# Expert weights in 16 KB pieces: which rows of the weights a partition holds, and the order in which turned rows take their columns

## The chip, the cores and the metric

The kernel runs on one core of a Trainium2 chip. The metric is the device time of one execution in microseconds. PE is TensorE (matmuls, with PEld for the loads of its stationary operand), DVE is VectorE, ACT ScalarE, POOL GpSimd and SP the engine that issues most DMAs. SBUF is the on-chip memory of 128 partitions; HBM is off the chip.

## What the reference computes

A decoder layer over 512 tokens of width 1024: a token mixer, a cross-attention, and then a hierarchical mixture of experts, which is what matters here. Everything is fp32.

```python
g_top, g_idx = lax.top_k(softmax(logits[:, :4]), 1)         # one of 4 groups
e_top, e_idx = lax.top_k(e_in, 2)                           # two of its 8 experts
combine = sum(one_hot(g_idx * 8 + e_idx, 32) * (softmax(e_top) * g_top))
for e in range(32):
    gate, up = split(t @ w_gate_up[e], 2)                   # (1024) x (1024, 2 * 512)
    y = (silu(gate) * up) @ w_down[e]                       # (512) x (512, 1024)
    out = out + combine[:, e] * y
```

## The kernel before, in words

The experts' phase (`expert_phase`, from about 838 us of the span) goes over the 32 experts in turn. Each expert has 64 slots; a token takes a slot of each of its two experts. For each expert:

- **gather** (line 1676): the 64 rows of the expert's tokens are picked out of `h_rows` by matmuls with a 0/1 matrix `sel`. The two halves of the model dimension go to the two halves of the output's partitions: the result has 128 rows (half, slot) and 512 columns. ACT copies it to `xr` (line 1828).
- **turn_rows** (line 1682): four PE transposes of 128 x 128 give it the model dimension on the partitions; ACT copies them to `xg[p, c, half, slot]` (line 1822). In a transpose the data (`xr`) is the stationary operand, which PE loads first, and the identity is the moving one.
- **gate_up** (line 1691): eight k-chunks, four from the transfer `lo` and four from `hi`, each in two halves of the output partitions.
- ACT and DVE form silu(gate) * up into `ee` (= `hh`); **turn_hidden** (line 1696) transposes it in two pieces, and ACT copies them back (line 1700).
- **down** (line 1706): four chunks of the hidden dimension, two halves each. ACT copies the result to `yy` (line 1834) and issues two DMAs that store it (line 1712). After the last expert, POOL fetches each token's two rows and they are summed and normed.

An fp32 matmul is two instructions on PE, a transpose one.

The order on PE is written out by hand (`tensor_main`): gate_up lo of expert e, turn_hidden of e-1, gate_up hi of e, turn_rows of e+1, gather of e+2, down of e-1. Experts 0 to 7 and 26 to 31 are straight code, the 18 between them a loop of six.

Weights lie in three sets of buffers (`WB = 3`) of three parts of 2 MiB: `lo`, `hi`, `down`, each of 128 partitions x 4 rows x 1024 columns. The names in the profile: set 0 is weights_0lo, weights_0hi, weights_0down, set 1 alike, set 2 is weights_2lo, `ring` and weights_2down. SP issues the loads (`sync_main`, `load_chunk`, line 1627): lo and hi of expert e+3 when gate_up of e is done, down of e+2 when down of e-1 is done. The loads of experts 0 to 2 are issued in the phase before, among loads of that phase's `w_co`. Expert e's matmuls wait on a semaphore for each part.

Before the change the row of `w_gate_up[e]` with number k * 128 + p lies in partition p, so that a partition's share of a transfer is four rows of 4 KB, each from another place, 512 KB apart. `xr[:, c * P:(c + 1) * P]` takes 128 columns side by side to match.

`overflow_pass` does the same work again for experts with more than 64 tokens; it uses the same functions, and no instruction of it runs with these inputs.

Of the kernel before, what the change touches and what calls it, by code (L numbers as in the profile page):

```python
# [12 lines left out]
P = 128  # L13
SEQ, D, MEM = 512, 1024, 256
NT, MT, KC = SEQ // P, MEM // P, D // P
# [1188 lines left out]
def cross_phase(nc, psum, g):  # L1204
# [4 lines left out]
    with ExitStack() as ctx:  # L1209
# [51 lines left out]
        @block.sync  # L1261
        def _(sp):
            def weights(n):
                sp.wait_ge(mm_done, n - 3)
                src = columns((g["w_out"], g["w_cq"], g["w_co"])[n // KC], n % KC)
                sp.dma_start(ring[:, n % 4], src).then_inc(landed[n % 4], 16)

            for n in range(4, 2 * KC):
                weights(n)
            load_gate_up(sp, g, 0, 0)  # L1270
            load_down(sp, g, 0, 0)
            for n in range(2 * KC, 2 * KC + 4):
                weights(n)
            load_chunk(sp, g, 1, 1, "down")
            load_chunk(sp, g, 1, 1, "gate_up_lo")
            sp.wait_ge(scores, XH)
            load_chunk(sp, g, 1, 1, "gate_up_hi")
            for n in range(2 * KC + 4, 3 * KC):
                weights(n)
            load_chunk(sp, g, 2, 2, "gate_up_lo")  # L1280
            sp.wait_ge(mm_done, 3 * KC)
            load_chunk(sp, g, 2, 2, "gate_up_hi")
            load_chunk(sp, g, 2, 2, "down")
# [333 lines left out]
            k.link(dve.tensor_copy(R["places"][:], places))  # L1617


CHUNKS = {"gate_up_lo": ("w_gate_up", 0, 0), "gate_up_hi": ("w_gate_up", 4, 1), "down": ("w_down", 0, 2)}  # L1620


def load_chunk(eng, g, e, w, name):

    source, k, at = CHUNKS[name]
    src = g[source][0].rearrange("e (k p) f -> e p k f", p=P)[bass.ds(e, 1), :, k:k + 4, :]
    eng.dma_start(g["weights"][w][at][:], src.rearrange("o p k f -> (o p) k f")).then_inc(g["weights_landed"][name][w], 16)


def load_gate_up(eng, g, e, w):  # L1630
# [8 lines left out]
def expert_phase(nc, psum, g):  # L1639

    ident, h_rows = g["ident"], g["h_rows"]
# [3 lines left out]
    with ExitStack() as ctx:  # L1645
        def sb(name, shape, dt=F32, c=ctx):
            return c.enter_context(nc.sbuf_tensor(name, shape, dt))
# [4 lines left out]
        weights = g["weights"]  # L1652
        sel = [sb(f"select{i}", [P, NT, SLOTS]) for i in range(2)]
        xr = sb("xr", [2 * SLOTS, D // 2])
        xg = [sb(f"xg{i}", [P, KC // 2, 2, SLOTS]) for i in range(2)]
        ee = [sb(f"ee{i}", [P, FF // 2]) for i in range(2)]
        hh = ee
# [21 lines left out]

        def turn_rows(pe, bank):  # L1680
            for c in range(KC // 2):
                mm = pe.transpose(bank[:, c * P:(c + 1) * P], xr[:, c * P:(c + 1) * P], ident[:])  # L1682
            return mm

        def gate_up(pe, q, w, bank, ks):
# [7 lines left out]

        def turn_hidden(pe, q, bank):
            for c in range(2):
                mm = pe.transpose(bank[:, c * P:(c + 1) * P], hh[q][:, c * P:(c + 1) * P], ident[:])  # L1696
            return mm

        def take_hidden(act, q, bank):
# [15 lines left out]
        with ExitStack() as inner:  # L1715
# [45 lines left out]
            def tensor_main(pe):  # L1761
# [6 lines left out]
                def rows_of(e):  # L1768
                    pe.wait_ge(xr_got, e + 1)
                    turn_rows(pe, G).then_inc(turned, 1)  # L1770
# [5 lines left out]
                def hidden_of(e, q):  # L1776

                    pe.wait_ge(hid, e + 1)

                    after(pe, hid_got, e - 1)  # L1780
                    turn_hidden(pe, q, T[q]).then_inc(hid_turned, 1)
# [403 lines left out]
```

## Time and profile before

| | us |
|---|---|
| median of 3 runs (lowest, highest) | 1360.67 (1359.71, 1362.56) |
| the profiled execution, its own time | 1361.83 |
| its span, first to last instruction | 1359.9 |
| PE busy | 1298.9 (96%) |
| DVE, ACT, POOL busy | 612.1, 393.7, 315.6 |
| granted clock of PE, mean | 0.986 |
| bytes moved by DMA | 282.93 MB, mean 208 GB/s |

Busy shares are means over stages with different limits. The page's slices divide the span into 40 parts of 34 us. The DMA share is the mean over 16 DMA engines; packets overlap a little, so that it can stand above 1. Ends of matmuls are modelled, and so the distance from the start of one group to the start of the next says more than the group's own length.

### The profile page before, as it was taken

The numbers are of one execution on the slowest core, as the hardware profiler recorded it, in microseconds if no ns is written. First come the engines' busy times: TensorE is split into PE (matmuls) and PEld (weight loads), VectorE is DVE, ScalarE is ACT, GpSimd is POOL, SyncE is SP. The second block draws the span as 40 slices with busy tenths as digits, with TensorE's granted clock in tenths as the row PEclk, the third lists the DMA queues.
The fourth block names the chain that finished last, engine by engine and source line by source line (L and its number), as shares of the span: only waits on it lengthen the run. The fifth ranks groups of instructions, "written<-read, shape, count | busy, mean of one in ns | idle before, by whom it ended". The sixth has DMA issues, their size and how long they took to land. (4 is left out here: it accounts for less than half of the span.)

```text
span 1359.9 us, 18136 instructions
## 1 busy us (share of the span) xinstructions
PE 1298.9 (96%) x6552; PEld 791.4 (58%) x6552; DVE 612.1 (45%) x1019; ACT 393.7 (29%) x951; POOL 315.6 (23%) x351
## 2 busy tenths in 40 slices
PE   7999999899989999999999999999999999999993
PEld 6788888798879888894455454333333333333321
DVE  4234888788968798860122214221122112211214
ACT  4023644445444626241101123111111111111112
POOL 2256654546555736211100000000000000000002
PEclk9999999999999999999999998999999999999997
DMA  6732221212212212404244523799999999999965
GB/s 214 252 98 78 79 62 48 64 47 65 77 34 76 62 47 71 147 32 144 77 158 140 213 93 124 296 416 421 419 420 420 421 420 421 421 420 420 420 277 209
DMA packets 165332, 282.93 MB, mean 208 GB/s; under 512 B 5928, under 2 KB 108557, under 8 KB 164493
## 3 DMA queue, kind: packets, MB, share of 16 engines
q1 hardware_dynamic: 156928, 265.83, 51.7%
q10 hardware_dynamic: 7181, 11.90, 2.4%
q0 software_dynamic: 1152, 4.19, 0.9%
q8 instruction: 52, 0.85, 0.2%
q14 instruction: 19, 0.16, 0.0%
HBM read 267.22 MB, written 14.68 MB: 207 GB/s over the span
## 5 line engine op out<-in xcount | busy, mean ns | idle before, releaser
L1906 DVE TENSOR_SCALAR ee<-ee 128x256 f32<-128x256 f32 x32 | 9.4, 294 | 366.7 <-ACT ee L1851 366.7
L1676 PE MATMUL bank<-kv_rows,select 128*64 128x512 f32 x512 | 118.8, 607 | 0.8 <-DVE select L1669 0.8
L2077 POOL DMA_INDIRECT weights_0lo<-expert_out,row x4 | 4.4, 1106 | 493.2 <-issue 493.2
L693 PE MATMUL bank<-h_sums,ring 128*128 128x256 f32 x384 | 91.1, 380 | 0.0
L693 PEld LDWEIGHTS bank<-h_sums,ring 128*128 128x128 f32 x384 | 71.9, 190 | 9.2
L1676 PEld LDWEIGHTS bank<-kv_rows,select 128*64 128x64 f32 x512 | 34.4, 138 | 63.8 <-issue 61.5
L693 PE MATMUL bank<-h_mix,weights_0lo 128*128 128x256 f32 x256 | 60.5, 390 | 6.1 <-issue 4.8
L693 PE MATMUL bank<-h_sums,weights_0hi 128*128 128x256 f32 x256 | 60.5, 379 | 0.0
L1307 PE MATMUL bank<-x_rows,ring 128*128 128x512 f32 x128 | 56.9, 607 | 3.1 <-PEq L459 3.1
L703 PE MATMUL bank<-weights_0lo,h_mix 128*128 128x128 f32 x512 | 58.9, 276 | 0.0
L1307 PE MATMUL bank<-weights_2down,ring 128*128 128x512 f32 x128 | 57.1, 597 | 1.7 <-DVE weights_2down L1507 1.7
L693 PEld LDWEIGHTS bank<-h_mix,weights_0lo 128*128 128x128 f32 x256 | 48.8, 195 | 16.6 <-issue 10.3
L703 PEld LDWEIGHTS bank<-weights_0lo,h_mix 128*128 128x128 f32 x512 | 57.9, 192 | 0.1
L1907 DVE RECIPROCAL ee<-ee 128x256 f32<-128x256 f32 x32 | 56.1, 1753 | 1.1
L1307 PE MATMUL bank<-weights_1lo,ring 128*128 128x512 f32 x128 | 56.1, 592 | 0.0
L879 ACT ACTIVATE ring<-bank 128x256 f32<-128x256 f32 x72 | 27.4, 381 | 98.6 <-PE bank L693 98.6
L759 PE MATMUL bank<-rr 128*128 128x64 f32 x448 | 53.2, 272 | 1.3 <-DVE aa L1131 1.3
L759 PEld LDWEIGHTS bank<-rr 128*128 128x128 f32 x448 | 52.7, 192 | 2.0 <-issue 1.6
L1482 DVE TENSOR_TENSOR x_t<-x_t,bank 128x512 f32<-128x512 f32 x16 | 11.0, 687 | 94.2 <-PE bank L1307 94.2
L693 PEld LDWEIGHTS bank<-h_sums,weights_0hi 128*128 128x128 f32 x256 | 48.6, 190 | 6.6
L1828 ACT ACTIVATE xr<-bank 128x512 f32<-128x512 f32 x32 | 19.1, 597 | 97.8 <-PE bank L1676 97.8
L1834 ACT ACTIVATE yy<-bank 128x512 f32<-128x512 f32 x32 | 19.1, 597 | 94.7 <-PE bank L1706 94.7
(350 smaller groups left out, 2484.6 us busy)
## 6 DMA issues: line engine op xcount, KB each, us to landing
weights_0lo<-in_w_gate_up SPq DMA_DIRECT2D x11, 2048.0 KB, 17.0
weights_0hi<-in_w_gate_up SPq DMA_DIRECT2D x11, 2048.0 KB, 21.4
weights_0down<-in_w_down SPq DMA_DIRECT2D x11, 2048.0 KB, 20.1
weights_1down<-in_w_down SPq DMA_DIRECT2D x11, 2048.0 KB, 20.7
weights_1lo<-in_w_gate_up SPq DMA_DIRECT2D x11, 2048.0 KB, 17.6
weights_1hi<-in_w_gate_up SPq DMA_DIRECT2D x11, 2048.0 KB, 22.0
weights_2lo<-in_w_gate_up SPq DMA_DIRECT2D x10, 2048.0 KB, 17.3
ring<-in_w_gate_up SPq DMA_DIRECT2D x10, 2048.0 KB, 21.7
```

The lines of the kernel that those rows point to most:

```text
L693: mm = pe.matmul(bank[:, 0:HALF_T], w[:, k], h[:, k], start=(fresh and k == 0), stop=(k == HALF_K - 1), skip_group_check=True)
L703: mm = pe.matmul(bank[:, cs], h_mix[:, k, cs], ring[2][:, k], start=(k == 0), stop=(k == KC - 1))
L759: mm = pe.matmul(bank[:, c0 + c * 64:c0 + c * 64 + 64], rr[l % 4][:, c * P:(c + 1) * P], rv, start=True, stop=True)
L879: act.activation(dst, bank, ACT.Copy).then_inc(taken, 1)
L1307: mm = pe.matmul(psum[n % 2][:], ring[:, n % 4, k], act[:, k], start=(k == 0), stop=(k == KC - 1))
L1482: dve.tensor_tensor(x_t[:, k], x_t[:, k], psum[n % 2][:], ALU.add).then_inc(evac, 1)
L1676: mm = pe.matmul(bank[half * SLOTS:(half + 1) * SLOTS, :], sel[q][:, t], h_rows[:, t, half * 512:(half + 1) * 512], start=(t == 0), stop=( ...
L1828: act.activation(xr[:], R_[:], ACT.Copy).then_inc(xr_got, 1)
L1834: act.activation(yy[q][:], Y[q][:], ACT.Copy).then_inc(y_got, 1)
L1906: st.link(dve.tensor_scalar(ee[q][:], ee[q][:], BIG, 1.0, ALU.min, ALU.add))
L1907: st.link(dve.reciprocal(ee[q][:], ee[q][:]))
L2077: pool.indirect_dma_start(out=y[:, t, :], out_offset=None, in_=table, in_offset=bass.IndirectOffsetOnAxis(ap=row[:, t:t + 1], axis=0)).the ...
```

## The change

Partition p now holds four rows of the weights that follow each other: for half h of `w_gate_up[e]`, rows h * 512 + 4p to h * 512 + 4p + 3, one piece of 16 KB in HBM and in SBUF. For `w_down[e]`, partition p holds rows u * 256 + 2p and the next one for u = 0 and 1, two pieces of 8 KB. The access patterns on both sides are written with the joined dimension last. Chunk c of the matmuls then contracts over the rows 4p + c, so the transposes take the columns c, c + 4, c + 8 and so on of `xr`, and the columns c, c + 2 and so on of `hh`. Nothing else is touched: as many DMAs and matmuls, in the same order, with the same waits.

```diff
-CHUNKS = {"gate_up_lo": ("w_gate_up", 0, 0), "gate_up_hi": ("w_gate_up", 4, 1), "down": ("w_down", 0, 2)}
+CHUNKS = {"gate_up_lo": ("w_gate_up", 0, 0), "gate_up_hi": ("w_gate_up", 1, 1), "down": ("w_down", None, 2)}
 
 def load_chunk(eng, g, e, w, name):
-    source, k, at = CHUNKS[name]
-    src = g[source][0].rearrange("e (k p) f -> e p k f", p=P)[bass.ds(e, 1), :, k:k + 4, :]
-    eng.dma_start(g["weights"][w][at][:], src.rearrange("o p k f -> (o p) k f")).then_inc(g["weights_landed"][name][w], 16)
+    source, half, at = CHUNKS[name]
+    dst = g["weights"][w][at][:]
+    if half is None:
+        src = g[source][0].rearrange("e (u p c) f -> e p u (c f)", u=2, c=2)[bass.ds(e, 1)].rearrange("o p u f -> (o p) u f")
+        dst = dst.rearrange("p (u c) f -> p u (c f)", u=2)
+    else:
+        src = g[source][0].rearrange("e (h p c) f -> e h p (c f)", h=2, c=4)[bass.ds(e, 1), half].rearrange("o p f -> (o p) f")
+        dst = dst.rearrange("p c f -> p (c f)")
+    eng.dma_start(dst, src).then_inc(g["weights_landed"][name][w], 16)
 
         def turn_rows(pe, bank):
             for c in range(KC // 2):
-                mm = pe.transpose(bank[:, c * P:(c + 1) * P], xr[:, c * P:(c + 1) * P], ident[:])
+                own = xr[:].rearrange("r (p c) -> r c p", c=KC // 2)
+                mm = pe.transpose(bank[:, c * P:(c + 1) * P], own[:, c], ident[:])
             return mm
 
         def turn_hidden(pe, q, bank):
             for c in range(2):
-                mm = pe.transpose(bank[:, c * P:(c + 1) * P], hh[q][:, c * P:(c + 1) * P], ident[:])
+                own = hh[q][:].rearrange("r (p c) -> r c p", c=2)
+                mm = pe.transpose(bank[:, c * P:(c + 1) * P], own[:, c], ident[:])
             return mm
```

## Rows read from the trace of the kernel before

**Rows 1.** The page's slices of 34 us: busy tenths of PE and DMA
```profile
PE   7999999899989999999999999999999999999993
DMA  6732221212212212404244523799999999999965
```
**Rows 2.** A stage of 45 us in the experts' phase: busy time of each engine
```profile
core 0: us, PE busy (x) PEld busy (x) DVE busy (x) ACT busy (x) POOL busy (x), PEclk, DMA share, GB/s
1000.00:1045.00 45.00, 45.00 (x214) 15.13 (x212) 9.69 (x15) 7.67 (x15) 0.00 (x0) 1.00 1.03 420
```
**Rows 3.** Waits of PE from 845 to 1318 us: total, times, longest
```profile
PE bank L1682 <- ACT xr L1828: 0.7, 1, 0.7
PE bank L1696 <- DVE ee L1910: 0.2, 1, 0.2
```
**Rows 4.** PE in order of time, one turn: start us, length us, group
```profile
883.25 3.65 PE L1676 MATMUL bank<-kv_rows,select 128*64 128x512 f32 x16
893.70 0.44 PE L1696 MATMUL bank<-ident,ee 128*128 128x128 f32 x2
894.07 3.65 PE L1691 MATMUL bank<-weights_0hi,xg 128*64 128x512 f32 x16
897.66 0.66 PE L1682 MATMUL bank<-ident,xr 128*128 128x128 f32 x4
898.24 3.22 PE L1676 MATMUL bank<-kv_rows,select 128*64 128x512 f32 x14
```
**Rows 5.** DMA issues of 856 to 870 and of 1270 to 1276 us: us to landing
```profile
weights_0lo<-in_w_gate_up SPq DMA_DIRECT2D x1, 2048.0 KB, 7.8
...
weights_1lo<-in_w_gate_up SPq DMA_DIRECT2D x1, 2048.0 KB, 24.1
```
**Rows 6.** SP's issue of expert 30's down, and its us to landing
```profile
1280.85 10.78 SPq L1627 DMA_DIRECT2D weights_0down<-in_w_down  x1
...
weights_0down<-in_w_down SPq DMA_DIRECT2D x1, 2048.0 KB, 29.4
```
**Rows 7.** PE in order of time, the last two down groups
```profile
1313.87 3.60 PE L1706 MATMUL bank<-weights_0down,ee 128*64 128x512 f32 x16
1320.66 5.29 PE L1706 MATMUL bank<-weights_1down,ee 128*64 128x512 f32 x16 [2.59 <-ACT ee L1700]
```
**Rows 8.** DMA packets while x_t is loaded, from 616 to 619 us
```profile
DMA packets 79, 1.29 MB, mean 431 GB/s; under 512 B 0, under 2 KB 0, under 8 KB 0
```
**Rows 9.** The stage from 704 to 716 us, columns as in rows 2
```profile
704.00:716.00 12.00, 12.00 (x38) 6.80 (x37) 2.07 (x3) 0.00 (x0) 0.00 (x0) 1.00 1.03 407
```
**Rows 10.** Line 1682: loads of the stationary operand, count and, ns min/median/max
```profile
L1682 PEld LDWEIGHTS bank<-ident,xr x128: 137/140/143, 845.1 to 1302.7; 128*128 128x128 f32 x128
```
**Rows 11.** VectorE: line 1131 from 421 to 436 us, and two contiguous groups
```profile
L1131 DVE TENSOR_TENSOR aa<-aa,tmp x7: 424/426/427, 422.8 to 435.1; 128x256 f32<-128x256 f32 x7
...
L1910 DVE TENSOR_TENSOR ee<-ee,bank 128x256 f32<-128x256 f32 x2 | 0.8, 420 | 0.1
L1586 DVE TENSOR_TENSOR r_c<-ln_c,geq 128x128 f32<-128x128 f32 x1 | 0.3, 291 | 0.0
```
**Rows 12.** VectorE reduces of 128 elements: ns min/median/max
```profile
L1587 DVE TENSOR_REDUCE e_in<-r_c x1: 378/378/378, 830.0 to 830.0; 128x32 f32<-128x128 f32 x1
L1877 DVE TENSOR_REDUCE at<-yy x2: 285/286/286, 839.9 to 841.7; 128x4 f32<-128x128 f32 x2
```
**Rows 13.** PE in order of time: line 759, last three levels, then first two
```profile
427.44 2.79 PE L759 MATMUL bank<-rr 128*128 128x64 f32 x24
...
408.48 1.90 PE L759 MATMUL bank<-rr 128*128 128x64 f32 x16
```
**Rows 14.** ACT in order of time, the last two stores and the hidden rows
```profile
1307.33 1.12 ACTq L1712 DMA_DIRECT2D expert_out<-yy  x2
...
1318.15 1.97 ACTq L1712 DMA_DIRECT2D expert_out<-yy  x2
1320.22 0.38 ACT L1700 ACTIVATE ee<-bank 128x256 f32<-128x256 f32 x1 [2.10 <-issue]
```

## The prediction

> **What bounds the kernel now.** I read the page's slices first. From slice 26 on, where the experts run, both PE and the DMA engines show nines [rows 1]; one of them waits for the other, or both are near their limits by chance. The stages' table says which: in 45 us PE is busy for all 45 at full clock, and the DMA share is 1.03, at 420 GB/s [rows 2]. The list of waits settles it. Between 845 and 1318 us PE waits for a tile twice, 0.7 and 0.2 us, and never for a weight transfer [rows 3]. PE's order of time shows one turn of one expert: gather at 883.25 us, next gather at 898.24, so 14.99 us, with every group starting where the last one stops [rows 4]. The chain that ended last gives PE's lines in this phase their whole length. So PE sets the end, and the DMA engines have a deadline to keep.
>
> How near is the deadline? One turn moves three transfers of 2.097 MB and two stores of 0.131 MB, 6.55 MB, and at 420 GB/s that takes 15.6 us. PE needs the next ones every 14.99 us. So the DMA engines fall behind by 0.6 us a turn, and live on the three buffers' head start. The landings show it: gate_up lo takes 7.8 us from issue at 856 us, and 24.1 at 1275 [rows 5]. SP's queue is then itself held up: the issue of expert 30's down takes 10.78 us [rows 6]. That transfer is issued at 1280.85 and lands 29.4 us later, at 1310.3; its first matmul is at 1313.87 [rows 6, 7]. So 3.6 us of slack are left at the tightest place.
>
> **The transfers.** Each 2 MiB load goes from 512 runs of 4 KB to 128 of 16 KB (down: 256 of 8 KB); 96 loads, no more and no fewer DMAs, on the same queue after the same waits. The kernel already has one load with such pieces, x_t from x_kept: in 3 us that hold only its packets, 79 of them carry 1.29 MB, 16.4 KB each, so a 16 KB piece goes as one packet, at 431 GB/s [rows 8]. That is 2.6% above the 420. At 431 a turn's bytes take 15.2 us instead of 15.6. PE waits for no transfer, so this takes nothing off the path: cost 0, gain 0, hidden by PE's matmuls. The cover is the 3.6 us; it would rather grow. From below: SP's hold-ups and ACT's late store (below) could give some 3 us at the very most (rival 3). From above: if the large pieces went no better than the worst full stretch of the trace, the 407 GB/s of 704 to 716 us [rows 9], the load would be the bound (rival 2).
>
> **The turned rows.** Four transposes a turn read xr, the data as the stationary operand, and two read the hidden rows; the change gives the first a step of 4 elements (16 B) and the second a step of 2 (8 B). Over 32 experts that is 128 [rows 10] and 64 instructions, all on PE's unbroken chain. The four take 897.66 to 898.24, 0.58 us, and the two 893.70 to 894.07, 0.37 us [rows 4]: two more cost 0.21, so one transpose costs 105 ns, on 0.16 of fixed lead. Nothing hides a slower one, as PE has no idle time to absorb it, and the matmuls queued behind it are the next gather and the next four k-chunks.
>
> What a step costs a stationary load no row shows, since every one of before is contiguous. The nearest rows are VectorE's. A step of 2 elements in SBUF: line 1131 adds in place over runs of 64, 32 and so on down to single elements at a step of 2 (8 B), seven levels, and one head's seven take 424 to 427 ns [rows 11]. So 8 B is free there, and I take 0 for the 64 hidden transposes (bounds 0 and 64 x 105 = 6.7 us, if they doubled). A large step: the reduce of line 1587 reads 128 elements in steps of 8 (32 B) and takes 378 ns; the reduce of line 1877, 128 elements in order, takes 286 [rows 12]. 92 ns over 128 elements are 0.72 ns each; on VectorE's own 1.04 (128x256 in 420 ns against 128x128 in 291, 129 ns for 128 elements, about 1.0) that is some 1.76 ns for an element that has a place of its own [rows 11, 12]. (It writes 32 results and the other 4, so part of the 92 may be that.) For 128 columns of xr: adding 92 ns to 105 gives 128 x 0.092 = 11.8 us; the full 1.76 ns, 225 ns in place of 105, gives 128 x 0.120 = 15.4; nothing gives 0. I take what lies between the first two, a doubling, +105 ns: 128 x 0.105 = **13.4 us**. Below nothing there is no reason: no column is left out.
>
> The Trainium skill, SBUF — State Buffer, section "Door 1: The DMA port swizzle", says lines of SBUF have 16 bytes and want at least two hits each for full rate. By that rule xr's columns (one hit) pay and the hidden ones (two) don't, which is how the two VectorE rows fall; it gives no price for TensorE. Against it stands TensorE: Matmul & The Clock Gate, section "LDWEIGHTS", by which a load takes its columns over 1.2 GHz, 107 ns for 128, whatever else; the trace's 105 agrees for contiguous columns, and by it alone the change would cost nothing, which is rival 1.
>
> The slower turn, 14.99 + 0.42 = 15.41 us, also gives the loads more time than their 15.2, so the backlog stops growing: nothing else becomes late.
>
> **Sum.** The profiled execution took 1361.83 us, span 1359.9 and 1.9 around it. 1361.83 + 13.4 = 1375.2. The median of the runs, 1360.67, stands 1.16 below, so I forecast **1374.1 us**.
>
> **Rivals.**
> 1. *Not slower: the strided load is free.* Its place is the four transposes. For it: PE's two-pass fp32 matmul streams 512 columns against two half arrays in 0.43 us for a pair [rows 4], and a load of 128 columns in 0.105 is 0.82 ns a column, slow for an array at full clock, so a slower fetch may fit under it; line 759's last levels move columns in steps of 2 and 24 of them take 2.79 us, 116 ns each, no more than the 16 of the contiguous levels in 1.90 (119) [rows 13]. Against it: those are 64 columns and 8 B. It decides if a line takes under 0.82 ns to fetch; every ns a column above that costs 128 x 128 ns = 16 us. Time 1360.7.
> 2. *The loads become the bound.* 128 pieces are 8 for each of 16 engines, so one slow engine holds a whole load, and a store on ACT's queue waits behind pieces of 0.6 us (16.4 KB at 431/16). For it: the row at 407 [rows 9]. Against: 431 with just such pieces [rows 8]. Price at 407: 29 turns of 6.55 MB are 190 MB, 467 us against 452, 14.5 later, less the 3.6 of slack: +11, 1371.6, if the transposes stay free; with the dearer ones it hides among them. It decides from 0.8% below 420.
> 3. *Faster.* At the end ACT issues a store for 1.97 us at 1318.15, where the others take 1.12, and the last hidden rows wait 2.10 us behind it [rows 14]; PE idles 2.59 us and its last 16 matmuls take 5.29 instead of 3.60 [rows 7]. If lighter queues shortened that issue by 0.85 us, and the matmuls behind the shorter pause kept their 3.60, it would give 0.85 + 1.69 = 2.5 us; with the 0.5 us by which SP's issues are longer than their least, once, 1357.7. Against: one store more or less late is all that speaks for it, and PE waits for no load.
>
> **Chances.** Forecast 0.52, rival 1 0.38, rival 2 0.05, rival 3 0.05. A difference under 0.2% (2.7 us) can't be told from none here. Slower than that: 0.52 + 0.05 = 0.57; within: 0.38; faster: 0.05. The forecast's own range, 11.8 to 15.4, is 1372.5 to 1376.1; with a little for the hidden rows 1377.5. As rival 1 holds more than 2 in 10, the range reaches down to it: 1360 to 1377.5.
>
> **What would show it.** The row transposes' slot, gather start less their start, at 1.0 us instead of 0.58, and the turn at 15.4; the hidden slot still 0.37. At 0.58 and 14.99 rival 1 holds. Weight packets of 16 KB; late landings of gate_up lo near 10 us if PE got slower, near 15 if not, and not 24. A wait of PE for a weight tile would show rival 2. I am wrong if the row slot is unchanged, or if the hidden slot grew too.

## The result, and the profile after

The changed kernel takes 1364.65 us (median of 19 runs, 1362.09 to 1367.84), the kernel before 1360.5 beside it (19 runs, 1358.75 to 1364.31): a ratio of 1.003, 95% interval 1.0022 to 1.0038, 4.15 us slower. The forecast was 1374.1. The profiled execution took 1366.23 us, with a span of 1364.2.

The page after first: a line of DMA issues (the last number is the median us to landing), and the count of packets.

```profile
DMA packets 132564, 282.93 MB, mean 207 GB/s; under 512 B 5928, under 2 KB 108557, under 8 KB 115341
...
weights_0lo<-in_w_gate_up SPq DMA_DIRECT2D x11, 2048.0 KB, 11.4
```

The change does what it says: the same 282.93 MB in 132,564 packets, 32,768 fewer than before: 384 for each of 64 gate_up loads and 256 for each of 32 down loads. The median landing of this tile was 17.0 us and is 11.4. The stage of [rows 2], with the same columns:

```profile
1000.00:1045.00 45.00, 45.00 (x210) 15.88 (x210) 9.69 (x15) 7.67 (x15) 0.00 (x0) 1.00 1.01 428
```

PE is still busy for all 45 us, and the DMA engines move 428 GB/s instead of 420. One turn on PE, in the columns of [rows 4]:

```profile
883.82 3.65 PE L1682 MATMUL bank<-kv_rows,select 128*64 128x512 f32 x16
...
894.27 0.50 PE L1704 MATMUL bank<-ident,ee 128*128 128x128 f32 x2
894.70 3.65 PE L1698 MATMUL bank<-weights_0hi,xg 128*64 128x512 f32 x16
898.29 0.75 PE L1689 MATMUL bank<-ident,xr 128*128 128x128 f32 x4
898.97 3.65 PE L1682 MATMUL bank<-kv_rows,select 128*64 128x512 f32 x16
```

From gather to gather it is 15.15 us where [rows 4] have 14.99. The row slot (898.29 to 898.97) grew from 0.58 to 0.68 us, the hidden slot (894.27 to 894.70) from 0.37 to 0.43, and no other slot of the turn changed: 0.16 us a turn, 5.1 us over 32. The loads of the stationary operand in these slots, as in [rows 10] (ns min/median/max):

```profile
L1689 PEld LDWEIGHTS bank<-ident,xr x128: 196/211/218, 845.1 to 1307.7; 128*128 128x128 f32 x128
...
L1704 PEld LDWEIGHTS bank<-ident,ee x64: 194/206/218, 864.0 to 1322.8; 128*128 128x128 f32 x64
```

Each takes some 70 ns more than the 140 of before, at a step of 16 B and of 8 B alike. The waits of PE from 845 to 1330 us, as in [rows 3]:

```profile
PE bank L1714 <- ACT ee L1708: 2.4, 1, 2.4
PE bank L1689 <- ACT xr L1836: 0.7, 1, 0.7
PE bank L1704 <- DVE ee L1918: 0.2, 1, 0.2
```

None is for a weight transfer. The last down group, against [rows 7]:

```profile
1325.56 5.07 PE L1714 MATMUL bank<-weights_1down,ee 128*64 128x512 f32 x16 [2.35 <-ACT ee L1708]
```

It starts 4.9 us later than before, with a pause ahead of it of 2.35 us instead of 2.59 (ACT's issue of the store is 1.80 us, not 1.97 as in [rows 14]). Its matmuls take 5.07 us, not 5.29, and what follows them is 0.4 us shorter in this execution. That leaves 4.3 us more of span.

### The profile page after: what moved, and what is told of

Its sections match the earlier page's. It is cut to its first block and busy times, and to the rows that moved or that the text cites. A ratio compares the mean times of both kernels' runs of the same rounds, so it can differ in the third digit from the quotient of the medians.

```text
span 1364.2 us, 18136 instructions
## 1 busy us (share of the span) xinstructions
PE 1303.4 (96%) x6552; PEld 799.9 (59%) x6552; DVE 612.0 (45%) x1019; ACT 393.7 (29%) x951; POOL 315.2 (23%) x351
## 2 busy tenths in 40 slices
DMA packets 132564, 282.93 MB, mean 207 GB/s; under 512 B 5928, under 2 KB 108557, under 8 KB 115341
## 6 DMA issues: line engine op xcount, KB each, us to landing
weights_0lo<-in_w_gate_up SPq DMA_DIRECT2D x11, 2048.0 KB, 11.4
weights_2lo<-in_w_gate_up SPq DMA_DIRECT2D x10, 2048.0 KB, 11.4
```

## The experiments

**One half of the change at a time.** Three kernels ran beside each other. The first keeps the 16 KB pieces and turns rows and hidden rows with contiguous columns; its chunks meet rows of the weights that aren't theirs, at the same amount of work. The edit in `turn_rows`, and alike in `turn_hidden`:

```diff
-                mm = pe.transpose(bank[:, c * P:(c + 1) * P], own[:, c], ident[:])
+                mm = pe.transpose(bank[:, c * P:(c + 1) * P], xr[:, c * P:(c + 1) * P], ident[:])
```

> The 16 KB pieces alone: weights loaded as after the change, transposes with contiguous columns as before (so each chunk meets the wrong rows of the weights, and the output is not the reference's). Theory A, the whole 4.15 us come from the strided loads of the stationary operand and the pieces cost and give nothing on PE's path: turn 14.99 us, median 1360.5, ratio 1.000. Theory B, the pieces take a share of the loss (or give something back that the strided transposes eat): the time leaves 1360.5 by more than 1.5 us, and a PE group other than the transposes is longer.

Measured: 1361.06 us against 1360.82, ratio 1.0006 (0.9998 to 1.0015). The turn is 14.99 us. The same stage:

```profile
1000.00:1045.00 45.00, 45.00 (x214) 15.11 (x210) 9.69 (x15) 7.68 (x15) 0.00 (x0) 1.00 1.01 429
```

The larger pieces alone raise the rate to 429 GB/s and move the time by nothing that can be measured.

The second is the kernel before with the two transposes of the change, and its 4 KB rows of DMA.

> The strided transposes alone, 4 KB rows as before (again the chunks meet the wrong rows of the weights). Theory A: row slot 0.68 us, hidden slot 0.43, turn 15.15, 32 turns give +5.1 less what the tail gives back, median about 1364.7, ratio 1.003; the backlog grows by 0.44 us a turn instead of 0.6, so gate_up lo lands 18 to 20 us after issue at the end. Theory B: it is nearer to before than the full change, by whatever the pieces cost.

Measured: 1364.38 us, ratio 1.0025 (1.0017 to 1.0034). Its row slot on PE is 0.68 us:

```profile
899.80 0.75 PE L1683 MATMUL bank<-ident,xr 128*128 128x128 f32 x4
900.48 3.65 PE L1676 MATMUL bank<-kv_rows,select 128*64 128x512 f32 x16
```

The hidden slot is 0.44 and the turn 15.15, at 420 GB/s. So the loss is the transposes': 1.0006 and 1.0025 add up to the 1.003 of the whole, and PE's order of time, below, leaves nothing for the pieces.

The third keeps the pieces and the whole computation, and lets ACT and VectorE write the rows in the order that the weights want, so that PE reads contiguous columns:

```diff
+        def take_rows(act):
+            return act.activation(xr[:].rearrange("r (c p) -> r p c", c=KC // 2),
+                                  psum[1][:].rearrange("r (p c) -> r p c", c=KC // 2), ACT.Copy)
...
-                    act.activation(xr[:], R_[:], ACT.Copy).then_inc(xr_got, 1)
+                    take_rows(act).then_inc(xr_got, 1)
```

and likewise the exp of the gate and VectorE's two products, with c = 2.

> The 16 KB pieces with all PE reads contiguous: ACT writes xr in the order (c, p) while it copies it out of PSUM, and ACT's exp and VectorE's two products read PSUM in steps of 2 and leave the hidden rows in the order (c, p). The full computation. ACT and DVE wait for PE most of the time, so theory A expects them to hide it: turn 14.99, 1360.5 us, at most 0.5 more at the end for the last hidden rows. If writes or reads with a large step cost ACT more than its slack (97.8 us of idle before xr over 32 turns, 3 us a turn), PE waits for xg or xr and it is slower.

Measured: 1361.06 us, ratio 1.0002 (0.9992 to 1.0012), with a turn of 14.99 and a row slot of 0.59. ACT pays for it, in its copy:

```profile
L1701 ACT ACTIVATE xr<-bank x32: 1045/1076/1077, 845.8 to 1293.5; 128x512 f32<-128x512 f32 x32
```

The copy took 597 ns in order, and the exp went from 383 to 622; VectorE's products kept 424 and 420 ns. ACT sits idle for 98 us in all before those copies, so nothing of it reaches PE between the first expert and the last. At the two ends it does: PE's first wait for `xr` is 1.15 us instead of 0.70, and its wait for the last hidden rows 0.4 instead of 0.2. This is the best version with large pieces, and its time can't be told from the kernel before.

**Rows and hidden rows apart.** Two kernels with the old transfers, each with one of the two strided reads.

> Only turn_rows takes strided columns (step 4, 16 B); 4 KB loads and contiguous hidden transposes (the chunks meet the wrong rows of the weights). Theory A, a price of 0.06 us for the first load of a group, exposed, and 10 to 20 ns for each after it, whatever the step: row slot 0.68, hidden slot 0.37, turn 15.09, +3.2 us of 32 turns: 1363.9. Theory C, 16-byte lines decide and the hidden ones cost nothing: then this run has all of the change's loss, turn 15.15, 1364.6.

> Only turn_hidden takes strided columns (step 2, 8 B). Theory A: hidden slot 0.43, row slot 0.58, turn 15.05, +1.9 us: 1362.7. Theory C: 14.99 and 1360.8, no difference. The two runs' gains in the turn should add up to the 0.16 us of the whole.

Measured: rows alone 1362.87 us, ratio 1.0016 (1.0007 to 1.0025); hidden rows alone 1362.32, 1.0008 (0.9997 to 1.002, so the time by itself does not tell it from nothing). PE's order of time does. Rows alone, then hidden rows alone:

```profile
1002.99 0.75 PE L1683 MATMUL bank<-ident,xr 128*128 128x128 f32 x4
1003.67 0.65 PE L1676 MATMUL bank<-kv_rows,select 128*64 128x512 f32 x2
```

```profile
1013.16 0.51 PE L1697 MATMUL bank<-ident,ee 128*128 128x128 f32 x2
1013.60 0.65 PE L1691 MATMUL bank<-ring,xg 128*64 128x512 f32 x2
```

0.68 and 0.44 us, each with the other slot as it was before (0.37 and 0.59): +0.10 for four transposes, +0.07 for two. Doubling the number does not double the cost.

The same timelines give a measure of the whole phase that is much finer than the medians. From the start of the first row transposes to the start of the last hidden ones, in the profiled execution of each kernel:

| kernel | first row transposes, last hidden ones | us between |
|---|---|---|
| before | 845.08, 1317.63 | 472.55 |
| pieces alone | 843.30, 1315.85 | 472.55 |
| the change | 845.13, 1322.71 | 477.58 |
| transposes alone | 846.65, 1324.22 | 477.57 |
| rows alone | 844.43, 1320.03 | 475.60 |
| hidden rows alone | 843.95, 1318.54 | 474.59 |
| ACT writes in order | 846.88, 1319.67 | 472.79 |

The pieces change nothing to 0.01 us, and the +3.05 of the rows and +2.04 of the hidden rows make 5.09, against the +5.03 of the change. What scatters from one execution to the next is the rest: the phases before this stretch (843.3 to 846.9 us) and the end behind it (40.3 to 42.3 us). The medians grew by less than the slots each time: 4.15 us for 5.1, and with the transposes alone 3.6, whose interval ends at 4.6. Where the difference of some 1 us goes is open.

**What the pieces are worth once the loads bind.** A third store of 256 KB a turn, into a tensor that nobody reads, in the kernel before and in the one with contiguous transposes and large pieces:

```diff
+            act.dma_start(spare[row2(row), :], yy_q[:]).then_inc(stored, 16)
```

> The kernel before with one more store of 256 KB a turn into a tensor that nothing reads (the same output), so that a turn moves 6.81 MB. If the loads have a deadline as said (0.6 us of backlog a turn, 3.6 us left), 420 GB/s take 16.2 us against 14.99, 29 turns fall back by 35.6 us, less the 21 that the buffers' head start holds: +14.7, PE waits for weights near the end, 1375. If the slack is larger than I read it, less; at 0 the deadline is no deadline.

> The same extra store with 16 KB pieces and contiguous transposes (the chunks meet the wrong rows). At 426.5 GB/s, from this layout's stages, 6.81 MB take 15.97 us: 29 x 0.98 = 28.5, less 21: +7.5, 1368. That is 7 us less than with 4 KB rows: what the pieces are worth once the loads are the bound. Rival: stores suffer more behind large pieces (7.8 us to landing against 5.7), ACT waits for them, and the gain is eaten.

Measured: with 4 KB rows 1377.31 us, ratio 1.0122 (1.0108 to 1.0137); with 16 KB pieces 1370.53, 1.0076 (1.0061 to 1.0091). The 6.8 us between them are the 7 that were expected; both times are some 2.4 us above their own expectations (1375 and 1368). A late stage of the first and one of PE's waits, then the same of the second:

```profile
1200.00:1245.00 45.00, 42.36 (x198) 14.35 (x196) 6.81 (x12) 7.38 (x15) 0.00 (x0) 1.00 1.03 420
...
PE bank L1691 <- DMA weights_1hi<-in_w_gate_up: 5.4, 3, 2.4
```

```profile
1200.00:1245.00 45.00, 45.00 (x213) 15.11 (x210) 9.71 (x16) 7.67 (x15) 0.00 (x0) 1.00 1.01 427
...
PE bank L1712 <- issue: 4.5, 2, 2.5
```

The 4.5 us of the second, for which the profile names no releaser, are waits for weights too: the `down` of experts 29 and 30 are issued at 1266.02 and 1281.01 us and land 40.5 and 41.4 us later, and PE's groups start at 1306.60 and 1322.50, 0.1 us behind. With 3.8 us of this kind PE waits for weights for some 13 us in the first kernel, and for 6 in the second. In each of them one group of 16 matmuls behind such a pause took 5.3 us instead of 3.6, which the expectation had not counted. The deadline of the prediction is real: more bytes make PE wait for weights, and the 2% of rate then pays.

**The price of a step, by itself.** The next four kernels don't compute the layer; TensorE alone runs rows of instructions on data in SBUF.

> Not the layer: streams of 32 PE instructions each on data of no meaning, to measure the step's price by itself; the time of the run says nothing. Theory A (a fixed price for any step): a transpose every 105 ns with contiguous columns, every 125 with a step of 2, 3, 4, 8 or 16 alike. Theory C (lines of 16 bytes): steps of 2 and 3 as contiguous, 4 and more dearer and equal among themselves. Third, a rate that falls with the step. In two-pass matmuls with 64 moving columns the same rise per load; with 512 moving columns (0.43 us each pass) a strided stationary load is hidden. A strided moving operand: 0.83 ns a column if free, more if not.

PE in order of time, 32 transposes at steps of 1, 2, 3, 4 and 8 elements; then 64 instructions each with 512 moving columns: stationary at step 4, moving at steps 2, 4 and 8.

```profile
51.01 3.66 PE L49 MATMUL bank<-ident,wide 128*128 128x128 f32 x32
54.50 4.00 PE L51 MATMUL bank<-ident,wide 128*128 128x128 f32 x32
58.34 3.83 PE L53 MATMUL bank<-ident,wide 128*128 128x128 f32 x32
62.01 4.00 PE L55 MATMUL bank<-ident,wide 128*128 128x128 f32 x32
65.85 3.79 PE L57 MATMUL bank<-ident,wide 128*128 128x128 f32 x32
...
147.50 27.63 PE L73 MATMUL bank<-wide 128*128 128x512 f32 x64
174.96 28.96 PE L75 MATMUL bank<-wide 128*128 128x512 f32 x64
203.77 57.76 PE L77 MATMUL bank<-wide 128*128 128x512 f32 x64
261.34 58.92 PE L79 MATMUL bank<-wide 128*128 128x512 f32 x64
```

From start to start, a transpose takes 109 ns in order and 120, 115 and 120 at steps 2, 3 and 4, and 113 at 8 and 16: some 4 to 11 ns more, not the +105 of my forecast, and under the 125 expected here. With 512 moving columns the strided stationary load is hidden altogether (27.46 us over 64, 429 ns each), while a strided moving operand costs nothing much at step 2 (450 ns) and double at step 4 (900). The two-pass matmuls of 64 moving columns did not rise alike, as I had expected: 111 and 118 ns at steps 1 and 2, but 233 and 238 at 4 and 8. The granted clock of those two streams had fallen to 0.62 and 0.50, so the next kernel measures step 4 again.

But 10 ns four times are 0.04 us, and the row slot grew by 0.10. The next kernel puts groups between matmuls of 128 columns.

> Not the layer: groups of four transposes between two long matmuls, as in the kernel, with a step of 1, 2, 4 and 16; then groups of one; then the same product as a two-pass matmul. The stream of 32 showed 109 ns contiguous and 113 to 120 strided, but in the kernel four cost 0.10 us more. If the first load of a group is exposed: a group of four +0.10 us at any step, a group of one +0.06 or so. If the price were per transpose: +0.025 for one. Two-pass matmuls in the stream took 111 ns an instruction with steps 1, 118 with 2 and 233 with 4, and the clock fell in that part; here the filler keeps it up, so if the doubling is real a group of four (8 instructions) takes 0.9 us more at a step of 4, and at 3 tells where the edge is (12 B). Moving operand: 450 ns at step 2, 3 unknown, 900 at step 4.

Starts of a group and of the matmuls behind it: four transposes at step 1, four at step 4, one at step 4 with its load, then eight two-pass instructions at steps 3 and 4.

```profile
32.01 0.60 PE L53 MATMUL bank<-ident,wide 128*128 128x128 f32 x4
32.44 1.88 PE L48 MATMUL bank<-wide 128*128 128x512 f32 x4
...
58.08 0.63 PE L61 MATMUL bank<-ident,wide 128*128 128x128 f32 x4
58.55 1.88 PE L48 MATMUL bank<-wide 128*128 128x512 f32 x4
...
92.56 0.20 PEld L72 LDWEIGHTS bank<-ident,wide 128*128 128x128 f32 x1 [0.24 <-issue]
92.98 0.27 PE L72 MATMUL bank<-ident,wide 128*128 128x128 f32 x1
93.09 1.88 PE L48 MATMUL bank<-wide 128*128 128x512 f32 x4
...
138.57 1.49 PE L85 MATMUL bank<-ident,wide 128*128 128x128 f32 x8
139.90 1.88 PE L48 MATMUL bank<-wide 128*128 128x512 f32 x4
...
157.25 1.91 PE L89 MATMUL bank<-ident,wide 128*128 128x128 f32 x8
158.99 1.88 PE L48 MATMUL bank<-wide 128*128 128x512 f32 x4
```

Four take 0.43 and 0.47 us, where the layer has 0.58 and 0.68, and one takes 0.11 with or without a step: the expected 0.06 for a group's first load is missing here. Something of the layer was not in this kernel. I took it for the semaphore wait ahead of the transposes.

> Not the layer: groups of transposes between two 512-column matmuls, as in b2_groups, but with a semaphore wait, long met, ahead of the group's first load, ahead of the matmuls behind the group, or both. Theory (a strided load takes 70 ns longer, and that is exposed once for each group whose first load stands behind a wait, since it can then not be fetched under the matmul before): with the wait ahead of the group, four transposes at step 1 take 0.58 us to the next matmul as in the layer (0.43 without a wait), and at steps 2, 4 and 16 about 0.68; two take 0.37 and at steps 2 and 4 0.43 to 0.45; one takes 0.26 and at step 4 0.32 to 0.33 (0.11 and 0.11 without a wait). With the wait ahead of the following matmuls alone, step 4 costs no more over step 1 than the 0.04 of b2_groups, and with both 0.10 again. Rival (the 0.06 of the layer comes from something else there, such as the other engines' reads of xr or the DMA traffic): the wait ahead of the group shifts all steps alike, and step 4 stays 0.04 above step 1.

It is not that: with a wait that is long met ahead of the group, behind it, or both, every number stays: four at step 4 with the wait ahead start at 57.13 us, the matmuls behind them at 57.60.

The other difference is the shape of the neighbours. In [rows 4] all matmuls around a group are 128*64: two halves of 64 columns side by side.

```diff
-                    pe.matmul(banks[i % 4][:], data(1), wide[:, 512:1024], start=True, stop=True)
+                    for h in range(2):
+                        pe.matmul(banks[i % 4][h * 64:(h + 1) * 64, :], data(1, 64, h * 64), wide[:, 512:1024],
+                                  start=True, stop=True)
```

> Not the layer: b2_groups again, but the matmuls between the groups come as two halves of 64 columns, as all of the layer's do, in place of whole ones of 128. After b3_waits, where a wait long met exposed nothing, the theory is that the first load of a transpose covers all 128 columns and so can't be made under a matmul that still uses 64 of them: its 70 ns more are exposed once a group. Then four at step 1 take 0.58 us to the next matmul as in the layer (0.43 between whole ones), at steps 2, 4 and 16 about 0.68; two take 0.37 and 0.43; one takes 0.26, and at step 4 0.32. Met waits on both sides change nothing. Rival (the exposed part comes from the layer's own surroundings, such as DMA traffic or other engines on xr): 0.43, 0.47, and for one 0.11 and 0.11, as between whole matmuls.

Four at step 1, four at step 4, then one at step 1 and one at step 4 with its load, each with the start of what follows:

```profile
34.12 0.66 PE L59 MATMUL bank<-ident,wide 128*128 128x128 f32 x4
34.70 1.94 PE L54 MATMUL bank<-wide 128*64 128x512 f32 x8
...
64.21 0.75 PE L67 MATMUL bank<-ident,wide 128*128 128x128 f32 x4
64.89 1.94 PE L54 MATMUL bank<-wide 128*64 128x512 f32 x8
...
133.11 0.33 PE L87 MATMUL bank<-ident,wide 128*128 128x128 f32 x1
133.37 1.94 PE L54 MATMUL bank<-wide 128*64 128x512 f32 x8
...
145.87 0.20 PEld L91 LDWEIGHTS bank<-ident,wide 128*128 128x128 f32 x1 [0.81 <-issue]
145.87 0.39 PE L91 MATMUL bank<-ident,wide 128*128 128x128 f32 x1
146.18 1.94 PE L54 MATMUL bank<-wide 128*64 128x512 f32 x8
```

0.58 and 0.68, 0.26 and 0.31; two take 0.37 and 0.44; waits on both sides change nothing. These are the layer's slots to 0.01 us, without its DMA traffic, its other engines or its data. So next to matmuls in halves of 64 columns a full-width transpose is 0.15 us dearer in order (0.11 to 0.26 for a group of one), and its first strided load costs 0.05 to 0.06 more; each further one costs 0.01 to 0.02. (Four at step 16 take 0.65, under the 0.68 that was expected for every step.)

The records of the loads show where this comes from. Between whole matmuls the lone transpose's load stands at 92.56 us, beside the matmul ahead of it, 0.42 us before the transpose. Between halves load and transpose start together at 145.87, after 0.81 us without a load, so that the load is exposed. The layer's row slot does the same, first before the change, then after it:

```profile
897.65 0.42 PEld L1682 LDWEIGHTS bank<-ident,xr 128*128 128x128 f32 x4 [0.81 <-issue]
```

```profile
898.28 0.56 PEld L1689 LDWEIGHTS bank<-ident,xr 128*128 128x128 f32 x4 [0.81 <-issue]
```

In the kernel with halves a lone load took 138 ns in order and 196 at step 4, and the slot grew by the same 0.06 us. What holds the load back, the halves still in use or the change of tile shape as such, no run separates.

## Why the prediction was wrong

**The bound.** PE's time in an unbroken chain: right. PE is busy for all 45 us in every such stage of every run of the layer, but for the late ones of the run with small rows and more stores, and its slots carry the whole loss.

**The transfers at cost 0.** Right, and measured alone (1.0006). The 431 GB/s of [rows 8] was a fair price for the stage's 428 to 429, and the deadline was real: with more bytes the pieces brought 6.8 us. One sign was mis-stated: I expected late landings of gate_up lo near 10 us if PE got slower and near 15 if not. After the change the same transfer lands in 14.1 us, and with large pieces but an unchanged PE it took 18.9. Both are below the 24.1 of [rows 5]; the direction held, the values were 4 too low. With small rows and the slower PE it took 22.9, where I had expected 18 to 20.

**The price of the row transposes.** This is the step that failed: "Nothing hides a slower one", and with it the size of the term. I set +105 ns for each of 128 at a step of 16 B, 13.4 us, by VectorE's figures in [rows 11, 12]. Measured: +0.10 us for a group of four, 3.2 us over 32 groups. What VectorE pays for a step says nothing about a transpose's load. The load itself does take longer, 140 to 211 ns, but the load of the next transpose is made beside the matmul of the one before, so that only 10 ns of the 70 show in a stream. With the exposed first load that makes 25 ns a transpose, a quarter of my value. So part of a slower load is hidden, by the transpose ahead of it, although PE has no idle time. The measured time lies in the range that I stated, but that is no merit of the sum: the forecast's own range began at 1372.5, and only rival 1 took the lower bound to 1360.

**The hidden transposes at 0.** Wrong too: I held 8 B for free after [rows 11]. The load grows by the same 70 ns, and the slot by 0.06 to 0.07 us, 2.1 us over 32. The prediction named this as a sign against it. Both errors come from one thing, pricing by the step; in a transpose most of the price goes by the group, as the fixed lead of 0.16 us worked out from [rows 4] could have told: by the loads' records it is the first load, exposed, and a load that grows makes it grow.

**The Trainium skill's rule.** In SBUF — State Buffer, section "Door 1: The DMA port swizzle", lines of SBUF have 16 bytes and want two hits each for full rate. For PE's other reads the runs follow it: moving operands of 512 columns at steps 2, 3 and 4 take 450, 676 and 900 ns, which is as 0.5, 0.75 and 1 line for an element; step 8, still one line, takes 918. For the two-pass fp32 product with the identity the same steps take 118, 166 and 217 ns an instruction, against 111 in order. A transpose's load does not follow it (120, 115 and 120), nor the rule's free step of 8 B. Why it escapes, no run here shows.

**Rival 1, the strided load is free** (1360.7), is refuted: 1.0025 with an interval from 1.0017 for the transposes alone. It was yet nearer to the time than my forecast. Beside it, the Trainium skill, TensorE: Matmul & The Clock Gate, section "LDWEIGHTS", gives 107 ns for a load of 128 columns; the 109 ns of the stream in order agree, the strided 120 are not in it. One reading in this rival was off: a pair of half arrays takes 0.45 us in [rows 4] (16 instructions in 3.59), not 0.43. Nothing rested on it.

**Rivals 2 and 3** did not happen. PE waits for no weight tile. At the end ACT's issue was 0.17 us shorter and the last matmuls 0.22 us quicker, some 0.5 us in the direction of rival 3, which hoped for 3. The other runs make this chance, since neither goes with the pieces: that issue took 1.12 us with small rows and strided hidden rows, and 2.29 with large pieces alone. Nor does the pause decide the matmuls behind it: 1.50 us of pause were followed by 5.35 us (ACT's orders), 2.71 by 3.65 (the transposes alone).

**The sum as it should have been:** 32 x (0.10 + 0.06) = 5.1 us, against 5.03 in the phase's own stretch, 4.15 between the medians and 4.4 between the profiled executions.

## What to carry to other kernels

Price a changed access on the engine and the kind of instruction that makes it: the same step of 16 B doubled a moving operand, cost a transpose 10%, and a stationary load under 512 moving columns nothing. Look at what stands beside the instruction: a longer load shows only where it isn't covered, and here it is uncovered once for every group that a change of tile shape sets off. Where the effect is near the scatter of the runs, measure the stretch of the timeline that it is in. Larger DMA pieces bring nothing while PE sets the end, yet they are slack that can be had for next to nothing, as long as an idle engine and not PE puts the data in order.

## What the runs showed of the hardware that was not expected

- A transpose of 128x128 fp32 alone between matmuls takes 0.11 us if these are 128 columns wide, and 0.26 if they are pairs of 64.
- Stores on ACT's queue land later beside large pieces: 5.6 us before and 8.7 after between 1270 and 1300 us. Nothing waited for them here.
- SP's issue of expert 30's down goes with the size of the pieces. With small rows it takes 10.78 us in [rows 6] and 6.96 to 9.85 in the three other runs without the extra store; with large pieces it takes 0.38 in all three of them:

```profile
1284.85 0.38 SPq L1633 DMA_DIRECT2D weights_0down<-in_w_down  x1
```
